# Token sums of a seven-product matmul without the norm's root, five more chunks in that form, and a weight sum made by an adding DMA

## The reference

```python
h = _layer_norm(x) * (1.0 + sc2) + sh2                      # up1, 512 tokens
u = _causal_depthwise_conv(h @ w_up[l], conv_w[l], conv_b[l])
a, val = jnp.split(u, 2, axis=-1)
y = (jax.nn.silu(a) * val) @ w_down[l]
...
def rmsnorm(x, g):
    y = xf * lax.rsqrt(jnp.mean(xf * xf, axis=-1, keepdims=True) + EPS)
    return (y * g.astype(jnp.float32)).astype(x.dtype)
def swiglu(x, w_gate, w_up, w_down):
    return (jax.nn.silu(x @ w_gate) * (x @ w_up)) @ w_down
h = h + 0.5 * swiglu(rmsnorm(h, ffn1_norm[l]), ...)         # up2, 16 + 512 tokens
...
h = h + 0.5 * swiglu(rmsnorm(h, ffn2_norm[l]), ...)         # up3, 512 tokens
```

## Time and profile before

| | |
|---|---|
| median of 3 runs | 1900.29 us (1899.62 to 1901.18) |
| the profiled execution's own time | 1899.8 us |
| its span, first to last instruction | 1898.0 us |
| TensorE matmul busy, share of the span | 1863.7 us, 98% |
| VectorE, ScalarE, GpSimd busy | 1205.2, 805.2, 42.0 us |
| chain that ended last, TensorE's share | 93% |
| mean granted TensorE clock | 0.997 |

### The profile page before, as it was taken

The page is one execution under the profiler, slowest core; times in us unless marked ns, Lnnn a source line. Parts: engine busy times, 40 slices in busy tenths (PEclk is TensorE's granted clock), DMA queues, the critical chain, the costliest instruction groups (busy, mean ns, idle before and its releaser), DMA issues.

```text
span 1898.0 us, 27244 instructions
## 1 busy us (share of the span) xinstructions
PE 1863.7 (98%) x11591; PEld 1607.6 (85%) x11591; DVE 1205.2 (63%) x1510; ACT 805.2 (42%) x1117; POOL 42.0 (2%) x60
## 2 busy tenths in 40 slices
PE   8999999999999999999999999999999999999997
PEld 3788878867789888699999999888788888998997
DVE  8677743459568478577784765764454466784864
ACT  4544543336335244253452444554323333452532
POOL 0021000002000000000000000000000000000000
PEclk9999999999999999999999999999999999999998
DMA  8454423221232323212332332211122222332231
GB/s 335 159 180 163 148 95 107 89 92 64 85 110 95 111 89 111 67 68 78 103 111 90 110 112 92 89 46 45 67 89 89 94 101 72 111 114 102 97 112 45
DMA packets 42582, 196.29 MB, mean 103 GB/s; under 512 B 3792, under 2 KB 8944, under 8 KB 27616
## 3 DMA queue, kind: packets, MB, share of 16 engines
q1 hardware_dynamic: 36656, 173.55, 26.6%
q0 software_dynamic: 5808, 21.04, 3.4%
HBM read 192.48 MB, written 2.10 MB: 103 GB/s over the span
## 4 chain that ended last, share of the span: by engine, by line
PE 93%; DVE 4%; ACT 2%; issue 1%; DMA 0%; POOL 0%; DVEq 0%; ACTq 0%; POOLq 0%
PE PS L808 91%; PE PS L975 1%; DVE W_lo L2283 1%; ACT W_hi L1654 0%; DVE N L2937 0%; ACT N L1654 0%; DVE N L2932 0%; DVE N L2896 0%; DVE T L3023 0%; DVE N L2927 0%; ACT H_hi L1654 0%; ACT X L1654 0%; DMA X<-in_xT 0%; DVE N L2311 0%; PE PS L1267 0%
## 5 line engine op out<-in xcount | busy, mean ns | idle before, releaser
L808 PE MATMUL PS<-H_hi,W_hi 128*128 128x512 f32 (+2 forms) x1368 | 447.4, 345 | 5.3 <-POOL H_lo L792 2.4
L808 PE MATMUL PS<-H_lo,W_hi 128*128 128x512 f32 (+2 forms) x1368 | 446.5, 344 | 0.0
L808 PE MATMUL PS<-H_hi,W_lo 128*128 128x512 f32 (+2 forms) x1344 | 443.4, 347 | 0.0
L1654 ACT ACTIVATE W_hi<-W_raw 128x2048 fp32r<-128x2048 f32 (+3 forms) x158 | 289.7, 1835 | 336.4 <-PE PS L808 330.2
L2283 DVE TENSOR_TENSOR W_lo<-W_raw,W_hi 128x2048 fp32r<-128x2048 f32 (+2 forms) x112 | 248.4, 2218 | 122.7 <-ACT W_hi L1654 121.8
L808 PEld LDWEIGHTS PS<-H_hi,W_hi 128*128 128x128 f32 x1368 | 247.5, 188 | 41.2 <-issue 4.4
L808 PEld LDWEIGHTS PS<-H_lo,W_hi 128*128 128x128 f32 x1368 | 247.0, 188 | 32.3 <-issue 0.6
L808 PEld LDWEIGHTS PS<-H_hi,W_lo 128*128 128x128 f32 x1344 | 243.4, 188 | 30.9 <-issue 0.7
L808 PE MATMUL PS<-G_hi,W_hi 128*128 128x264 f32 (+2 forms) x736 | 216.7, 333 | 5.0 <-DVE W_lo L2283 4.6
L808 PE MATMUL PS<-G_lo,W_hi 128*128 128x264 f32 (+2 forms) x736 | 217.1, 334 | 0.0
L808 PE MATMUL PS<-G_hi,W_lo 128*128 128x264 f32 (+2 forms) x736 | 216.4, 333 | 0.0
(11 more groups left out here) (363 smaller groups left out, 3246.1 us busy)
## 6 DMA issues: line engine op xcount, KB each, us to landing
W_raw<-in_wts SPq DMA_DIRECT2D x116, 1024.0 KB, 4.9
ring<-in_wada POOLq DMA_DIRECT2D x32, 512.0 KB, 3.9
W_raw<-in_wdown SPq DMA_DIRECT2D x12, 1024.0 KB, 5.1
W_raw<-in_wdown SPq DMA_DIRECT2D x12, 768.0 KB, 4.4
W_raw<-in_wdown SPq DMA_DIRECT2D x12, 640.0 KB, 4.2
A_high<-in_wada SPq DMA_DIRECT2D x6, 1024.0 KB, 18.6
W_raw<-in_wdown SPq DMA_DIRECT2D x12, 384.0 KB, 4.7
X<-in_xT SPq DMA_DIRECT2D x4, 512.0 KB, 5.4
```

The costliest lines, as they stand in the source:

```text
L808: return nc.tensor.matmul(*a, **kw)
L1654: return nc.scalar.activation(*a, **kw)
```

## The change

Seven products start at pair 2 (the third) in all three stages: chunk 5 of up1, chunks 4 and 5 of up2 and up3 become fast, 45 fast chunks in place of 40. In up2 and up3 the token sums are made from x times gain (`gained` on ScalarE into XG), H stays as it is, and VectorE multiplies the result of each fast chunk by the root after `add_products` (`root_products`). The first weight sum is no longer an addition on VectorE: GpSimd's queue issues a DMA that reads the other weight quarter (128 x 4 x 128 floats) from memory and adds it to the quarter in `W_raw`, behind that chunk's load. `down_last` waits for chunk 33 only ahead of the third half-tile, and the sums of seven squares stand one half-tile later. The semaphore of a memset in the linear attention is merged with another.

```diff
-FAST_FROM = 3
+FAST_FROM = {"up1": 2, "up2": 2, "up3": 2}
...
+def rooted_before(name, n):
+    return fast_before(name, n) - fast_before("up2", 0)
...
+        def summed_at(name, n):
+            done = fast_before(name, n)
+            return sem(f"first_sum{done % 2}"), 16 * (done // 2 + 1)
...
@ gpsimd
+            def first_sums(name):
+                for n, (_, i, k) in enumerate(FFN):
+                    if not is_fast(name, n):
+                        continue
+                    c = At(st[name].c + n)
+                    of = wts[WTS_AT[name] + 2 * i + k].rearrange("p (h k m n) -> p h k m n", h=2, m=2, n=P)
+                    pool.wait_ge(w_loaded[c.odd], (c.half + 1) * 16)
+                    pool.dma_start(quarter(W_raw, c.odd, 1, 0), of[:, 1, :, 1], accum_op=ALU.add
+                                   ).then_inc(summed_at(name, n)[0], 16)
+            first_sums("up1")
+            first_sums("up2")
             pool.wait_ge(w_used, st["back"].c)
...
             pool.wait_ge(sem("mix_const_loaded"), 64)
+            first_sums("up3")
@ tensor, down_last
                 for q in (2, 3):
                     chunk_ready(At(s.c + down_at(2, q)))
                     group_free(s, At(down_at(2, q)))
-                for k in range(KT // 2, KT):
-                    tile(0, k)
+                    tile(0, 2 * q)
+                    tile(0, 2 * q + 1)
+                tile(1, 4)
                 out_seven(0)
-                tile(1, 4)
                 out_last(0)
@ tensor, seven_products
-                if first and name != "up1":
-                    pe.wait_ge(sem("rerooted"), 2 * UPS.index(name) - 1)
...
-                if first and name != "up1":
-                    pe.wait_ge(sem("rerooted"), 2 * UPS.index(name))
@ scalar, ffn_split
                 if is_fast(name, n):
-                    act.wait_ge(sem("weight_sums"), 3 * fast_before(name, n) + 1)
+                    act.wait_ge(*summed_at(name, n))
@ scalar, up_first
                 ffn_split(name, 5)
+                round_weight_sums(name, 5)
                 hidden(1)
+                plain_base(2, 0)
+                snapshot(name, 5, 0, TB, SEQ)
                 ffn_split(name, 6)
-                plain_base(2, 0)
+                snapshot(name, 5, 1, TB, SEQ)
+                snapshot(name, 5, 2, TB, SEQ)
                 silu(2)
-                plain_base(2, 1)
@ scalar, up_second
+                def gained(ks):
+                    for k in ks:
+                        activate(XG[:, k, 0:tok], n_.src(k), ACT.Copy, scale=n_.gain(k)).then_inc(n_.sem("gained"), 1)
...
                 ffn_split(name, 2)
+                gained(range(4))
                 late_root(n_)
+                gained(range(4, KT))
                 silu(0)
+                ffn_split(name, 3)
                 hidden(0)
-                ffn_split(name, 3)
+                ffn_split(name, 4)
                 silu(1)
-                ffn_split(name, 4)
-                hidden(1)
-                ffn_split(name, 5)
-                silu(2)
-                ffn_split(name, 6)
+                round_weight_sums(name, 4)
+                for q in range(4):
+                    round_tile_sum(name, q, half)
...
-                for n in range(6, end):
+                for n in range(4, end):
...
-                    if n == 6:
-                        for q in range(4):
-                            round_tile_sum(name, q, half)
-                        reroot()
@ vector, weight_sums
-                dve.wait_ge(sem("weight_sums"), 3 * done + 1)
+                dve.wait_ge(*summed_at(name, n))
@ vector, up_first
                 plain_taps(1, 1)
+                weight_sums(name, 5)
                 product(1)
...
-                    if is_fast(name, n + 2):
-                        first_sum(name, n + 2)
@ vector, up_second
-                def root_tiles(ks):
...
-                def low_rerooted():
...
+                def root_products(n, to):
+                    dve.wait_ge(*freed_at(s, n))
+                    root = RS[:, 0:tok].rearrange("p (o t) -> p o t", o=1).to_broadcast([P, 2, tok])
+                    vector.tensor_tensor(to[:, :, 0:tok], to[:, :, 0:tok], root, ALU.mult).then_inc(sem("root_taken"), 1)
...
                 product(0)
+                ffn_split(name, 3)
                 low_hidden(name, 0, tok)
-                ffn_split(name, 3)
-                root_tiles(range(4))
+                dve.wait_ge(*n_.reach("gained", KT))
+                for _ in tile_sums(name, XG, half):
+                    pass
                 out(2)
+                weight_sums(name, 4)
                 ffn_split(name, 4)
-                root_tiles(range(4, KT))
-                out(3)
-                product(1)
...
+                low_tile_sums(name, half)
...
                     if is_fast(name, n - 1):
                         add_products(name, n - 1, up_tiles(name, j)[last], tok)
+                        root_products(n - 1, up_tiles(name, j)[last])
...
-                    if n == 7:
-                        low_rerooted()
-                    if is_fast(name, n + 2):
-                        first_sum(name, n + 2)
```

More of the change, by code:

```diff
@@ L78, in is_fast @@
 def is_fast(name, n):
-    return n < len(FFN) and FFN[n][0] == "up" and FFN[n][1] >= FAST_FROM and FFN[n][2] in FAST_PARTS[name]
+    return n < len(FFN) and FFN[n][0] == "up" and FFN[n][1] >= FAST_FROM[name] and FFN[n][2] in FAST_PARTS[name]
+def rooted_before(name, n):
+    return fast_before(name, n) - fast_before("up2", 0)
 def fast_before(name, n):
@@ L246, in build_program @@
         with ExitStack() as over:
-            sb("rooted_below", [P, 4 * KT * TOK], FP32, over)
-            NR = sb("NR", [P, KT, TOK], FP32, over)
+            sb("gained_below", [P, 4 * KT * TOK], FP32, over)
+            XG = sb("XG", [P, KT, TOK], FP32, over)
         with ExitStack() as over:
@@ L456, in count @@
                     return PAIR_COUNTS[self.number - 1].get(what, 0)
-                if what == "rooted":
+                if what == "gained":
                     return KT if self.number in (4, 6) else 0
@@ L583, in up_tiles @@
         def up_tiles(name, i):
-            if name == "up1" or i < FAST_FROM:
+            if name == "up1" or i < FAST_FROM[name]:
                 return TA, TB
-            j = 2 * (i - FAST_FROM)
+            j = 2 * (i - FAST_FROM[name])
             return (TA, TB, TC)[j % 3], (TA, TB, TC)[(j + 1) % 3]
         def hidden_tile(name, i):
-            return TC if name == "up1" or i < FAST_FROM else up_tiles(name, i)[1]
+            return TC if name == "up1" or i < FAST_FROM[name] else up_tiles(name, i)[1]
         def hidden_slots(i):
@@ L2073, in silu @@
                 def silu(i):
-                    act.wait_ge(*freed_at(s, up_at(i, 0)))
+                    if i < FAST_FROM[name]:
+                        act.wait_ge(*freed_at(s, up_at(i, 0)))
+                    else:
+                        act.wait_ge(sem("root_taken"), rooted_before(name, up_at(i, 0)) + 1)
                     gate = up_tiles(name, i)[0]
@@ L2079, in hidden @@
                     round_hidden(name, i, tok)
[L2081 to L2085, removed]
+                def gained(ks):
+                    for k in ks:
+                        activate(XG[:, k, 0:tok], n_.src(k), ACT.Copy, scale=n_.gain(k)).then_inc(n_.sem("gained"), 1)
                 def tile_free(i, k):
-                    if k == 0 and i > FAST_FROM:
+                    if k == 0 and i > FAST_FROM[name]:
                         act.wait_ge(sem("hidden_lo"), HIDDEN[name] + i - 1)
@@ L3044, in product @@
                 def product(i):
-                    if i < FAST_FROM:
+                    if i < FAST_FROM[name]:
                         dve.wait_ge(*freed_at(s, up_at(i, 1)))
                     else:
-                        dve.wait_ge(sem("shifted"), KT + 2 * (i - FAST_FROM + 1))
+                        dve.wait_ge(sem("shifted"), KT + 2 * (i - FAST_FROM[name] + 1))
                     dve.wait_ge(sem("hidden_silu"), HIDDEN[name] + i + 1)
-                    up = TB if i < FAST_FROM else TC
+                    up = TB if i < FAST_FROM[name] else TC
                     vector.tensor_tensor(TC[:, :, 0:SEQ], TA[:, :, 0:SEQ], up[:, :, 0:SEQ], ALU.mult).then_inc(sem("hidden_prod"), 1)
@@ L3122, in product @@
                     gate, up = up_tiles(name, i)
-                    dve.wait_ge(*freed_at(s, up_at(i, 1)))
+                    if i < FAST_FROM[name]:
+                        dve.wait_ge(*freed_at(s, up_at(i, 1)))
+                    else:
+                        dve.wait_ge(sem("root_taken"), rooted_before(name, up_at(i, 1)) + 1)
                     dve.wait_ge(sem("hidden_silu"), HIDDEN[name] + i + 1)
@@ L3147, in up_second @@
                 product(0)
+                ffn_split(name, 3)
                 low_hidden(name, 0, tok)
-                ffn_split(name, 3)
-                root_tiles(range(4))
```

(15 more changed lines are left out.)

35 lines of the change are left out of this document (9 added, 26 removed).

## The result

The changed kernel takes 1890.56 us (median of 5 runs, 1889.86 to 1890.84) against 1900.29: a ratio of 0.9949, 95% interval 0.9936 to 0.9962. The forecast was 1891.2. The profiled execution has a span 9.6 us shorter than before.

The account below looks back on a forecast made before the run. TensorE, busy nearly throughout, was taken as the bound. Gains of 6.9 + 7.3 = 14.2 us less losses of 5.2 leave 9, so 1891.2 us was forecast, range 1887.5 to 1897.5.

Parts of the forecast that it names:

- The tail: In down_last, the 4.59 us wait, 1.7 of slow clock and 0.85 wait for square sums go: 7.3 us gained.
- Five chunks: Seven products in chunk 5 of up1 and chunks 4 and 5 of up2 and up3 save TensorE 6.9 us.
- The root: VectorE's root_products make six product chunks late in up3 and up2: 1.8 and 0.6 us lost; first passes lose more.
- The chain named: In product chunks: add, root, weight sums, product, W_lo, WS_lo, TensorE's next chunk; in up3 9.96 us against 9.88.
- The head: Start of up3: four gained tiles ahead of ScalarE's Sqrt make it late for TensorE, 0.4 us lost (0.2 to 0.6).
- Rival C: VectorE becomes the pace of up2 and up3, each late hand-over costing 0.7 us: 1897; chance 0.12.
- The adding DMA: Each fast chunk's 256 KB adding transfer on GpSimd's queue takes 5 us, has about 8 of room, and is hidden.
- Rival A: The adding DMA is late beyond 8 us after its load; at 8.75 the gain of 9 is gone; chance 0.06.
- Rival B: VectorE's two-input instructions hold up the adding DMA's issue, 4 us more, 16 us lost: 1907; chance 0.03.
- the mild half: For GpSimd's DMAs: VectorE's addition of two tensors takes no exclusive port lock, only competes with GpSimd's reads; sum unchanged.
- the strict half: VectorE's 2-port modes lock the port pair shared with GpSimd and starve its DMA descriptors; 16 us would be lost.
- Rival D: The tail keeps a wait because VectorE's square sums or a bank hold early half-tiles: 7.3 becomes 1, 1897.5; chance 0.07.

Follow-up runs that it names:

- the two experiments: The kernel before with only down_last's new order: 1892.18 us; the changed kernel with down_last's old order: 1898.12 us.
- the one with two pieces: The changed kernel with the adding DMA in two halves of 128 KB, the second issued when the first has landed: 1909.53 us.

## Why the prediction came out right

- **The tail:** right in kind, a little small. 7.3 was forecast between 5.3 and 7.9; 7.9 came in the trace, 8.0 and 7.6 in the two experiments. The prediction took the waits from the idle times in brackets, which count from a modelled end; by starts its terms are larger. In the kernel before, TensorE's timeline has, on either side of the start at 1862.01:

```profile
1857.03 0.39 PE L808 MATMUL PS<-G_hi,W_lo 128*128 128x512 f32 x1
...
1866.40 0.28 PE L808 MATMUL PS<-G_hi,W_lo 128*128 128x256 f32 x1
```

  The wait is 1862.01 - 1857.03 = 4.98 in place of the 0.23 of such a matmul, so 4.75 and not 4.59. The 21 steps to 1866.40 take 4.39 in place of 21 x 0.118 = 2.48, so the slow clock is 1.9 and not 1.7. The sums of squares start 1.12 after the matmul ahead of them (1875.28 to 1876.40) in place of 0.12, so 1.0 and not 0.85. Together 7.65; 0.25 stays open.
- **Five chunks:** the 6.9 gained and the 5.2 given back nearly cancel, as forecast (net 1.7; 2.0 with everything but the tail). up1: forecast 0 with a G_lo wait of 1.8, which was 1.6; measured 0.07 in the trace and 0.2 the other way with chunk 5 plain.
- **The root:** 0.31 in each of six chunks of up3 (forecast 0.3) and 0.08 in each of six in up2 (0.49 in all; forecast 0.1 each, 0.6 in all). The chain named was the right one: with the root behind WS_lo both losses are gone. The small waits for WS_lo that the profile after was to show stand in no waits view, only in the starts of TensorE. The first passes of up2 and up3 cost 0.53 and 0.65 by the kernel without the root (its adds on either side stand 45.41 and 43.41 us apart, those of the changed kernel 45.93 and 44.06), forecast 0.4 and 0.6.
- **The head:** 0.38 for the Sqrt behind four gained tiles, forecast 0.4.
- **Removing first_sum shortens no chain:** shown twice. Rival C, VectorE as the pace, was further off than its chance of 0.12 says: VectorE does all this work and the first sum too at 9.87 per chunk.
- **The adding DMA: hidden, but the room was wrong.** The sum took 4.4 (forecast 5, which was right), but "about 8 us" came from the median landing of loads in the kernel before, 4.9, and from the steady part. Beside the new transfers a load in up3's steady part took 6.0 in the changed kernel and 6.3 in the one with two pieces, which leaves 6.8 and 6.6, and the tightest places are the starts of the second passes, where VectorE has no product chunk ahead of it and the transfer itself took 7.2 in up2 and 5.4 in up3: 0.24 to spare in the one, 0.27 too late in the other. That this cost nothing was luck; the prediction had not looked there. Rival A was much nearer than a chance of 0.06 says; its point of 8.75 was too high, as sums that came 7.2 to 8.0 behind their loads in up3's steady part, and 12.2 at the start of up2's second pass, cost 19 us.
- **Rival B** falls in this kernel: transfers issued while VectorE was busy 18.56 of 20.05 us (the window 1659.17 to 1679.22) landed in 4.3 to 4.6. This agrees with the mild half of the rule of the Trainium skill, SBUF — State Buffer, "Who interferes with whom", for additions of two tensors; VectorE ran nothing but operations of two tensors in that window, so it says nothing of the strict half. **Rival D** falls too: no wait stands ahead of the half-tiles.

## What to carry to other kernels

Give the last work of a bound engine to the inputs that are ready first: eight half-tiles in another order were worth four times as much as five chunks of fewer matmuls. Ahead of adding an instruction to an engine with idle time, find the chain it lengthens and try it behind the last hand-over of that chain; here the root's place was worth 2.7 of the 4.1 us that it cost. The room of a transfer is read at every start of a loop as well as in its steady part, and with the landing times that the new traffic leaves.

## What was not expected of the hardware

An adding transfer of 256 KB in pieces of 512 bytes landed in 4.4 us (median), of 128 KB in 3.4 and of 64 KB in 2.7, so halves one behind the other came 7.2 to 8.0 behind their load in up3's steady part; at the starts of the second passes, with the next 1 MB load under way, a whole one took 7.2 and 5.4. GpSimd was busy 1276 ns for each issue, against 544 for a 512 KB load of the ring. VectorE at 19.91 of 20.05 us was still not the pace, since its instructions start before the recorded end of the one ahead.
